# First rows and constants loaded earlier, and the modulation's columns transposed on the chip, in a hybrid RG-LRU, attention and expert layer

## What is computed

```
silu_c, silu_cc = silu(c), silu(c_ctx)
m_lat = silu_c  @ w_mod + b_mod            # 1024 x 6144
m_ctx = silu_cc @ w_mod + b_mod
sh1, sc1, g1, sh2, sc2, g2 = split(m_lat, 6)      # and sh1c, sc1c, ... of m_ctx
h_lat = normalise(x)   * (1 + sc1)  + sh1         # mean and variance over the 1024 columns
h_ctx = normalise(ctx) * (1 + sc1c) + sh1c
u, g, q, k, v = split(h @ w_in)                   # w_in: 1024 x 1792
```

## Time and profile before

| | |
|---|---|
| median of 3 runs | 2081.2 us (2080.24 to 2082.03) |
| the profiled execution | 2081.28 us |
| its span, first to last instruction | 2079.5 us |
| mean granted TensorE clock | 0.923 |
| PE busy | 1713.2 us, 82% of the span |
| DVE busy | 1464.5 us, 70% |
| ACT busy | 1066.5 us, 51% |
| DMA moved | 412.59 MB, 198 GB/s in the mean |

### The profile page before, as it was taken

The page is one execution under the profiler, slowest core; times in us unless marked ns, Lnnn a source line. Parts: engine busy times, 40 slices in busy tenths (PEclk is TensorE's granted clock), DMA queues, the critical chain, the costliest instruction groups (busy, mean ns, idle before and its releaser), DMA issues. The chain is left out here.

```text
span 2079.5 us, 76106 instructions
## 1 busy us (share of the span) xinstructions
PE 1713.2 (82%) x31174; PEld 1373.2 (66%) x31176; DVE 1464.5 (70%) x1828; ACT 1066.5 (51%) x1378; POOL 526.5 (25%) x413
## 2 busy tenths in 40 slices
PE   3488888888669997899961689986899799999947
PEld 0266666434257776455541689986899799999932
DVE  2466766388869997788878747777888636578727
ACT  2234343577558886433311535566676435456626
POOL 0000000000047777333322113231323121233213
PEclk7599999999889999899975899998999899999979
DMA  9321211367363331344326576898999748879837
GB/s 375 104 92 56 96 60 52 129 229 259 122 251 124 115 121 40 125 153 159 136 91 223 196 242 206 266 361 316 352 373 342 263 137 280 270 228 368 272 77 278
DMA packets 167293, 412.59 MB, mean 198 GB/s; under 512 B 15977, under 2 KB 24625, under 8 KB 165553
## 3 DMA queue, kind: packets, MB, share of 16 engines
q1 hardware_dynamic: 155554, 369.14, 49.4%
q0 software_dynamic: 11664, 42.47, 8.3%
HBM read 343.38 MB, written 68.19 MB: 198 GB/s over the span
## 5 line engine op out<-in xcount | busy, mean ns | idle before, releaser
L2200 PE MATMUL ps<-arena 128*128 128x64 f16 x7680 | 708.5, 195 | 53.9 <-DVE arena L2121 25.7
L2200 PEld LDWEIGHTS ps<-arena 128*128 128x128 f16 x7680 | 686.5, 99 | 62.5 <-issue 50.4
L2201 PE MATMUL ps<-arena 128*128 128x64 f16 x7680 | 708.3, 195 | 4.7 <-issue 3.9
L2202 PE MATMUL ps<-arena 128*128 128x64 f16 x7680 | 708.2, 195 | 3.9 <-issue 3.0
L2201 PEld LDWEIGHTS ps<-arena 128*128 128x128 f16 x7680 | 686.2, 99 | 6.0 <-issue 5.0
L2202 PEld LDWEIGHTS ps<-arena 128*128 128x128 f16 x7680 | 686.3, 99 | 2.8 <-issue 2.7
L2121 DVE SCALAR_TENSOR_TENSOR arena<-arena 128x2048 f16<-128x2048 f32 (+1 forms) x232 | 457.6, 2012 | 162.9 <-ACT arena L2048 95.5
L2048 ACT ACTIVATE arena<-arena 128x2048 f16<-128x2048 f32 x192 | 359.0, 1904 | 126.3 <-DMA arena<-w 80.0
L644 PE MATMUL ps<-arena 128*128 128x256 f16 (+1 forms) x1680 | 237.7, 303 | 21.1 <-DVE arena L529 21.1
L644 PEld LDWEIGHTS ps<-arena 128*128 128x128 f16 x1680 | 165.8, 100 | 87.3 <-DVE arena L529 15.2
L2015 POOL COPY ix<-gidx 128x1 int32 (+1 forms) x40 | 47.0, 1176 | 531.3 <-DVE arena L2154 531.3
(11 more groups left out here) (308 smaller groups left out, 3107.6 us busy)
## 6 DMA issues: line engine op xcount, KB each, us to landing
arena<-w SPq DMA_DIRECT2D x192, 1024.0 KB, 12.0
arena<-hT_d SPq DMA_DIRECT2D x64, 512.0 KB, 6.2
arena<-w_mod SPq DMA_DIRECT2D x16, 1536.0 KB, 8.3
h_d<-arena SPq DMA_DIRECT2D x17, 512.0 KB, 3.0
x_d<-arena SPq DMA_DIRECT2D x17, 512.0 KB, 2.6
arena<-x SPq DMA_DIRECT2D x8, 1024.0 KB, 6.2
hT_d<-arena SPq DMA_DIRECT2D x16, 512.0 KB, 3.1
arena<-x SPq DMA_DIRECT2D x16, 512.0 KB, 4.7
```

The costliest lines, as they stand in the source:

```text
L2200: pe.matmul(out, whi[lane][:, at:at + P], high, start=first, stop=False)
L2201: pe.matmul(out, whi[lane][:, at:at + P], low, start=False, stop=False)
L2202: return pe.matmul(out, wlo[lane][:, at:at + P], high, start=False, stop=last)
```

## The change

In `phase_modulation`:

- The ring's fourth slot, the raw `w_in` and the rows lie elsewhere in `arena`, so that the places of the context rows, the first x rows, the parameters and the tables are free in this phase.
- `w_in` is loaded in twelve transfers (four groups of k, of 2, 2, 3 and 1, by three ranges of columns); ScalarE starts when the groups with k = 0 to 3 have landed. The two zero transfers are issued ahead of the second round of slabs.
- The stationary side of the modulation's matmuls is padded with zeros to 32 columns, so that all 128 PSUM partitions are written, and the additions of `b_mod` run once for each half over 128 partitions, after all eight slabs. The place of the rows is zeroed first, and `b_mod` is loaded after that.
- Behind the last slab SyncE issues the context rows, the first x rows, the parameters, and the tables.
- DVE makes all eight low halves of `w_in` first, then takes the statistics of the context rows, adds `b_mod`, scales the context rows, and forms `mcol` from PSUM, where PE has put six transposes of the rows. POOL makes the first power in this phase.
- The stores to `mod_rows` are issued when the rows are done, and their landing is awaited only in the phase of the output projection.

In `phase_project` those loads, the reading back of `mod_rows`, the first norm and the small transpose are gone. A semaphore in the expert phase is replaced by one that an earlier phase used.

```diff
 def phase_modulation(nc, env):
-    a = arena_slices(arena, 0, [(f"w{j}", 2 * WIDE) for j in range(RING)] + [("rows", HALVES * NARROW), ("spare", D)])
+    ring = [arena[:, at:at + 2 * WIDE].rearrange("p (k n) -> p k n", k=2) for at in (0, 2 * WIDE, 4 * WIDE, PAR0 + 36)]
+    rows = arena[:, ROWS0:ROWS0 + HALVES * NARROW]
-    c2a = small[:, 2 * KD:4 * KD]
+    c2a = small[:, 384:384 + 32 * KD]
         def _(sp):
             sp.dma_start(c2s, g["c2"]).then_inc(c_ld, 16)
+            sp.wait_ge(rows_done, 1)
             for m in range(4):
-                sp.dma_start(rows[m], by_group[0][m]).then_inc(c_ld, 16)
+                sp.dma_start(row_of[m], by_group[0][m]).then_inc(c_ld, 16)
...
-            for dst, src in ((0, 0), (D_RNN, D), (REST, D_RNN)):
-                size = QKV if src == D else D_RNN
-                sp.dma_start(raw[:, :, dst:dst + size], w_in[:, :, src:src + size]).then_inc(win_ld, 16)
+            first = 0
+            for at, count in RAW:
+                part = arena[:, at:at + count * D_IN].rearrange("p (k n) -> p k n", k=count)
+                for dst, src in ((0, 0), (D_RNN, D), (REST, D_RNN)):
+                    size = QKV if src == D else D_RNN
+                    sp.dma_start(part[:, :, dst:dst + size], w_in[:, first:first + count, src:src + size])\
+                        .then_inc(win_ld if first < KD // 2 else win_ld2, 16)
+                first += count
+            sp.wait_ge(rows_done, 2)
+            for table in (g["h2_d"], g["x1_d"]):
+                sp.dma_start(table[SEQ:SEQ + P, :], spare).then_inc(rows_st, 16)
             for n in range(RING, RING * HALVES):
                 sp.wait_ge(mod_mm, n - RING + 1)
                 sp.dma_start(ring[n % RING], slab(n)).then_inc(wmod_ld[n % RING], 16)
-            sp.wait_ge(rows_done, 1)
-            for table in (g["h2_d"], g["x1_d"]):
-                sp.dma_start(table[SEQ:SEQ + P, :], spare).then_inc(rows_st, 16)
-            sp.wait_ge(rows_done, 1 + 4 * HALVES)
+            sp.wait_ge(later("b_pads"), START + 1)
+            sp.dma_start(first_rows(arena, 0), g["ctx_x"].rearrange("(t p) d -> p t d", p=P)).then_inc(x_ld[0], 16)
+            sp.dma_start(first_rows(arena, 1), g["x"][0:TPC * P, :].rearrange("(t p) d -> p t d", p=P)).then_inc(x_ld[1], 16)
+            sp.dma_start(arena[:, PAR0:PAR0 + C_RNN * NPAR].rearrange("p (c n) -> p c n", n=NPAR),
+                         g["rg_par"].rearrange("(c p) n -> p c n", p=P)).then_inc(tab_ld, 16)
+            for at, src in ((COS0, "cos_t"), (SIN0, "sin_t")):
+                sp.dma_start(arena[:, at:at + T_LAT * 32].rearrange("p (n d) -> p n d", d=32), g[src].rearrange("n p d -> p n d"))\
+                    .then_inc(tab_ld, 16)
+            sp.wait_ge(rows_st, 32)
+            sp.wait_ge(rows_done, 2 + HALVES)
             for m in range(4):
-                sp.dma_start(by_group[1][m], rows[m]).then_inc(rows_st, 16)
-            sp.wait_ge(rows_st, 96)
+                sp.dma_start(by_group[1][m], row_of[m]).then_inc(rows_st, 16)
...
         def _(pe):
-                            mm = pe.matmul(ps[32 * m:32 * m + 2, i, 0:NARROW], c2a[:, 2 * k:2 * k + 2],
+                            mm = pe.matmul(ps[32 * m:32 * m + 32, i, 0:NARROW], c2a[:, 32 * k:32 * k + 32],
...
+            pe.wait_ge(rows_done, 2 + HALVES)
+            for i in range(HALVES):
+                for q in range(COLS):
+                    mm = pe.transpose(ps[:, 2 + i, q * P:(q + 1) * P], rows[:, i * NARROW + q * P:i * NARROW + (q + 1) * P], g["idn"][:])
+            mm.then_inc(later("b_mcol_tr"), 1)
         def _(dve):
+            nc.vector.memset(rows, 0.0).then_inc(rows_done, 1)
+            nc.vector.memset(c2a, 0.0)
             nc.vector.memset(spare, 0.0).then_inc(rows_done, 1)
+            for k in range(KD):
+                dve.wait_ge(win_hi, 2 * k + 2)
+                for cols, (high, low) in halves:
+                    nc.vector.scalar_tensor_tensor(low[:, k, :], raw[k][:, cols], W_SCALE, high[:, k, :], ALU.mult, ALU.subtract)
+            scale = norm_rows(nc, dve, g, first_rows(arena, 0), 0, (x_ld[0], START + 16))
             dve.wait_ge(c_ld, 80)
+            dve.wait_ge(mod_mm, RING * HALVES)
             for i in range(HALVES):
-                dve.wait_ge(mod_mm, RING * (i + 1))
-                for m in range(4):
-                    nc.vector.tensor_tensor(rows[m][:, i, :], ps[32 * m:32 * m + 2, i, 0:NARROW], rows[m][:, i, :], ALU.add).then_inc(rows_done, 1)
-                for k in range(4 * i, 4 * i + 4):
-                    dve.wait_ge(win_hi, 2 * k + 2)
-                    for cols, (high, low) in halves:
-                        nc.vector.scalar_tensor_tensor(low[:, k, :], raw[:, k, cols], W_SCALE, high[:, k, :], ALU.mult, ALU.subtract)
+                part = rows[:, i * NARROW:(i + 1) * NARROW]
+                nc.vector.tensor_tensor(part, ps[:, i, 0:NARROW], part, ALU.add).then_inc(rows_done, 1)
+            scale()
+            dve.wait_ge(later("b_mcol_tr"), START + 1)
+            for s in range(2):
+                at = ps[:, 2:4, 0:NARROW].rearrange("p i (q m c) -> p c i m q", q=COLS, m=4)[:, s]
+                nc.vector.tensor_scalar(mcol[:, s, 0:12].rearrange("p (m q) -> p m q", q=COLS), at[:, 0], X_SCALE, None, ALU.mult)\
+                    .then_inc(sc_ok, 1)
+                nc.vector.tensor_scalar(mcol[:, s, 12:15], at[:, 1, 0], X_SCALE, None, ALU.mult).then_inc(sc_ok, 1)
+                nc.vector.tensor_scalar(mcol[:, s, 15:16], at[:, 1, 1, 0:1], X_SCALE, None, ALU.mult).then_inc(sc_ok, 1)
+            dve.wait_ge(sc_ok, START + 6)
+            nc.vector.tensor_scalar(mcol[:, :, KD:2 * KD], mcol[:, :, KD:2 * KD], X_SCALE, None, ALU.add).then_inc(sc_ok, 1)
```

More of the change, by code:

```diff
@@ L200, in output_weights, with first_rows, norm_columns, norm_rows @@
                                         ("wr", KD * 36), ("br", 36), ("whi", KD * D // 2), ("wlo", KD * D // 2)])
+X_FIRST = B0
+COS0 = B0 + 2 * TPC * D + 4 * (KD * CHUNK // 2) + 4 * CHUNK
+SIN0 = COS0 + T_LAT * 32
+RAW = ((15204, 2), (X_FIRST + 2 * TPC * D, 2), (SIN0 + T_LAT * 32, 3), (9216, 1))
+ROWS0 = WIN0 - 1300
+assert PAR0 >= RAW[3][0] + D_IN and RAW[0][0] + 2 * D_IN + 4 <= B0 and RAW[1][0] + 2 * D_IN + D <= COS0
+assert RAW[2][0] + 3 * D_IN <= ROWS0
+def first_rows(arena, j):
+    return arena[:, X_FIRST + j * TPC * D:X_FIRST + (j + 1) * TPC * D].rearrange("p (t d) -> p t d", t=TPC)
+def norm_columns(small):
+    return dict(mcol=small[:, 0:32].rearrange("p (s n) -> p s n", s=2),
+                st=small[:, 32:32 + 12 * TPC].rearrange("p (t a s) -> p t a s", t=TPC, a=2),
+                mv=small[:, 80:80 + 2 * TPC].rearrange("p (t s) -> p t s", t=TPC),
+                ve=small[:, 96:96 + TPC], rs=small[:, 100:100 + TPC], mh=small[:, 104:104 + TPC])
+def norm_rows(nc, dve, g, x, s, landed):
+    sem, col = g["sem"], norm_columns(g["small"])
+    stats, var_e, rstd, normed = sem("b_stats"), sem("b_var"), sem("b_rstd"), sem("b_normed")
+    st, mv, ve, rs = col["st"], col["mv"], col["ve"], col["rs"]
+    dve.wait_ge(landed[0], landed[1])
+    for t in range(TPC):
+        for a in range(2):
+            nc.vector.bn_stats(st[:, t, a, :], x[:, t, a * 512:(a + 1) * 512]).then_inc(stats, 1)
+    dve.wait_ge(stats, START + 3 * TPC * s + 2 * TPC)
+    dve.sem_inc(g["alone"], 1)
+    for t in range(TPC):
+        nc.vector.bn_aggr(mv[:, t, :], st[:, t, :, :]).then_inc(stats, 1)
+    dve.wait_ge(stats, START + 3 * TPC * s + 3 * TPC)
+    nc.vector.tensor_scalar(ve, mv[:, :, 1], EPS, None, ALU.add).then_inc(var_e, 1)
+    def scale():
+        dve.wait_ge(rstd, START + s + 1)
+        for t in range(TPC):
+            nc.vector.tensor_scalar(x[:, t, :], x[:, t, :], mv[:, t, 0:1], rs[:, t:t + 1], ALU.subtract, ALU.mult).then_inc(normed, 1)
+    return scale
 def phase_modulation(nc, env):
@@ L208, in phase_modulation @@
     HALVES = FRONT // WIDE
+    COLS = NARROW // P
     def slab(n):
@@ L214, in phase_modulation @@
     sem, arena, ps, small = g["plain_sem"], g["arena"], g["ps"], g["small"]
+    later = g["sem"]
     c_ld, silu_done = sem("a_c_ld"), sem("a_silu_done")
@@ L261, in _ @@
                 pool.sem_inc(s, START)
+            nc.gpsimd.memset(col["mh"], -0.5).then_inc(later("b_pads"), 1)
+            pool.wait_ge(later("b_pads"), START + 1)
+            pool.wait_ge(later("b_var"), START + 1)
+            nc.gpsimd.tensor_tensor(col["rs"], col["ve"], col["mh"], ALU.pow).then_inc(later("b_rstd"), 1)
         @block.scalar
@@ L489, in _ @@
         def _(pool):
-            nc.gpsimd.memset(mh, -0.5).then_inc(pads, 1)
             k_words = arena[:, KT0:V0].rearrange("p (z t) -> p z t", z=2 * NKV)
@@ L499, in _ @@
             pool.wait_ge(pads, START + 8)
-            with pool.Fori(0, LAST + 1) as s:
+            with pool.Fori(1, LAST + 1) as s:
                 pool.wait_ge(var_e, START + s + 1)
@@ L1005, in _ @@
             sp.dma_start(ow["gnc"], g["gn"]).then_inc(w_ld, 16)
```

(1 more changed line is left out.)

78 lines of the change are left out of this document (30 added, 48 removed).

## The result

In the first comparison the changed kernel took 2060.49 us (median of 5; 2054.13 to 2062.72) and the kernel before 2080.24 (median of 5; 2070.84 to 2082.03): a ratio of 0.9913, interval 0.9884 to 0.9941.

| | before, median (n) | after, median (n) | ratio | interval |
|---|---|---|---|---|
| first | 2080.24 (5) | 2060.49 (5) | 0.9913 | 0.9884 to 0.9941 |
| second | 2075.96 (29) | 2059.37 (6) | 0.9931 | 0.9915 to 0.9947 |
| third | 2068.55 (23) | 2057.06 (5) | 0.9933 | 0.9909 to 0.9957 |
| fourth | 2078.55 (15) | 2060.84 (6) | 0.9923 | 0.9906 to 0.9940 |

A forecast was written before the change was run, and what follows sets the result against it. DMA engines bound everything up to 55.3 us, then short steps follow one another. Terms from the last slab at 57.0 put the first modulated tile at 68.2 instead of 81.48, 13.3 us less: 2068.0 us, range 2064.0 to 2074.0.

The forecast's parts named there:

- the tile: Start of ScalarE's first modulated tile (L424) in the projection: 81.48 us before, forecast 68.2, 13.3 us less.
- How the numbers follow: Prediction's section on chances and range: forecast 0.79, range 2064.0 to 2074.0 us, faster by more than 4.2 us 0.95.
- Zero rows: Two 512 KB writes moved ahead of the second round of slabs: last slab +1.0 us later, bounds +0 and +1.65.
- Twelve transfers of `w_in`: Splitting the w_in load costs 0, bounds -0.5 and +2.7 us; as a rival at +2.7, 2070.7 us, chance 0.05.
- Halves: w_in conversions start near 31 us, last low half ends near 49; the second 8.10 us leave the path.
- Context rows: Loads issued directly behind the last slab: the context's 1024 KB need 2.5 us, land at 59.5 and start DVE's chain.
- the rival that loads behind the slab are served together with it: Context, x and tables hold up the last slab until 63.3: 2071.4 us, or 2074.5 if context lands last; chance 0.08.
- Additions: Adding b_mod on DVE: two of 128x384 instead of eight of 2x384, 0.58 each, 1.15 us, ending at 63.8.
- Tables: Cosine and sine loads become the wait at the first low half after L424: 2068.7 or 2072.7 us, chance 0.04.
- trail the slabs: Rival: w_in's halves still come behind the modulation slabs, returning 8.1 us: 2076 us, chance 0.01.
- The clock: PE's rise to full clock early in the projection: counted 0, with 2.9 us kept both ways.
- The slower rival: Projection stays longer at half clock: gain gone after 26.6 us more, 2086 us at 36 more; chance 0.03.

The follow-up runs named there:

- The variant: Changed kernel with the two zero-row transfers issued behind the first x rows; run three times: 13.9, 17.6 and 16.4 us less than the kernel before.
- the columns through memory: Changed kernel with loads early, but the rows stored, awaited, read back and transposed as in the kernel before: 12.3 us less than the kernel before.
- low halves early alone: Kernel before with w_in in two groups of k and all low halves ahead of the second additions: 4.3 us less than the kernel before.

## Why the prediction was wrong, and where it was right

**The step that failed** is the one from the tile to the time, under "Sum" and "How the numbers follow". The saving at the tile, 12.83 us, is within 0.5 of the 13.3 forecast. But the time was worked out as 2081.2 less that saving, as if 2081.2 held for the kernel before within the 1.8 us of the three executions that I was shown, and with nothing for what lies behind the tile ("After L424 the diff changes nothing that costs time"). Neither had a term in the range, which ended with the bounds of the front's own terms.

By the means of the first comparison the 8 us that are missing divide as follows. The kernel before took 2078.0 and not 2081.2, which is 3.2 us. The changed kernel took 2059.9, that is 18.1 less; with 12.8 at the tile, 5.3 lie behind it. The tile itself gives back 0.5. Of the 5.3 the later comparisons confirm 1.8 with an error of 0.8, whose cause is open (above); the rest is within the error of 2.6 that the difference of two means of five has here. So part of the miss is chance. The scatter is plain from the runs: the kernel before has a standard deviation of 3 to 5 us within a comparison (2062.6 to 2084.0 over all), and medians of 2068.6 to 2080.2 from chip to chip. A sign of it stood in the profile too, though only later profiles made it readable: it has the longest experts' phase of the 17. A range for a median of five should have had about 5 us more at either end, twice that error, and would have held 2060.5.

**Point by point at the front:**

- Start: b_mod issued at 1.70 (1.8 forecast), the stream 0.50 later (0.62). Right.
- Zero rows: forecast +1.0 with an upper bound of 1.65; the last slab's matmuls began at 58.17, that is 2.33 later than the start explains. The variant shows that it is the zero rows: behind x they leave the slab at 55.68. The term was 2.5 by size and rate, less 0.85 that the last slab seemed to have paid already (4.61 us behind the third against 3.76), and both parts are off. The first slabs of the round show the whole price: 46.88 is 3.17 later than 43.21 plus the start, and in the other three profiles of the change the same sum gives 2.8 to 3.1. And the 0.85 is not particular to the zero rows. In the variant, with the context rows behind it, the last slab still came 4.55 us after the third (4.37 and 4.47 in the other two profiles). With the zero rows ahead it was 3.79, 3.79, 3.96 and 4.28 in the four profiles of the change, and 4.72 with the columns through memory. What causes this lateness stays open; as a credit it was not safe.
- Twelve transfers of `w_in`: 0 forecast; the conversions of the second part begin at 39.63, 0.21 after the 39.42 of before in a stream that is 0.50 late. Right. The 2.7 us by the section "Bandwidth" of "DMA: Bandwidth & Descriptors" of the Trainium skill did not come: its rate for a transfer of 1 MB did not hold for these, one behind the other in a full queue.
- Halves: conversions at 30.32 (31 forecast) and 39.63 (40), last low half done at 49.55 (49). Right.
- Context rows: 2.54 us behind the last slab (2.5). Right, so the rival that loads behind the slab are served together with it, which put the slab at up to 63.3, fell.
- Additions 1.02 us (1.15), transposes 1.51 (1.7), columns 66.45 to 67.16, 0.71 (1.1, outside the bounds of 0.8 to 1.3): together 0.7 us cheaper, which gave back part of the zero rows' 1.3. The six small operations began 0.06 to 0.09 us apart and the last 0.18 behind the sixth, below even my lower bound. That the tile came out within 0.5 is thus in part two errors that offset each other.
- SyncE: the sine table's issue ended at 63.27, the stores at 66.01, ahead of DVE's 67.16. DVE set the end, as forecast, with a margin of 1.2 us.
- End of the phase at 67.45 (66.9), first tile at 68.65 (68.2). The recorded terms, summed from 59.5, give 66.55 for the columns' end where the text has 66.65, and 68.04 for the tile, rounded there to 68.2.
- Tables: the first low half (L599, 69.80) waited for ScalarE's tile and not for the tables, so that rival fell too; and with conversions from 30.32 and the last low half at 49.55 the halves don't trail the slabs.
- The clock: the first 72 projection matmuls took 10.32 us (10.89 before), 0.6 less, within the 2.9. Full clock was granted within the window 81 to 82, as forecast. The slower rival fell: the rest of the projection took 300.7 us against 301.2.

## What to carry to other kernels

When a stretch is bound by a full DMA queue, count every transfer that moves ahead of the awaited one with its whole size over the rate, and take nothing off for a delay whose cause is not shown. Taking work off the last engine of a phase pays only down to the next. With low halves early alone that was SyncE's wait for stores to land, 2.4 us behind DVE, and only removing the trip through memory as well set it free; with the zero rows behind x it was SyncE's issue of the stores, which took 0.6 of the 2.3 us hoped for. And a forecast of a time needs the scatter of executions as a term of its own, and one for what the change might do where it is thought to do nothing: a saving that the timeline placed to half a microsecond was forecast in a time that was 7.5 us off.

## What the runs showed of the hardware

- Which of its two levels TensorE has in the first 60 us does not follow from the program alone: 16 equal matmuls took 2.79 us in one slab and 1.50 in the next, and the same slab of the same program, the one at about 50.6 us, took 2.79 us in the changed kernel's first profile and 1.50 in its second; in the fourth all of them took 2.79. This agrees with the Trainium skill, "TensorE: Matmul & The Clock Gate", section "What's actually happening", by which the chip's look at activity runs on by itself and does not start with the kernel. In the projection full clock came 5.9 and 5.7 us after the first matmul in the two profiles of before, and 4.7, 4.2, 4.7 and 6.0 us after it in the four of after. The granted clock of a window ahead of the first record is shown as 1.00: in the kernel before the windows up to 23 us show it while the slab at 20.57 took 2.74 us, so that there the durations, not the clock column, tell the level.
- Four memsets of 128x3072 on DVE, one behind the other, took 2.62 us each and left 0.59 us of idle between them; of the three memsets of 768, 256 and 1024 columns at the start of the changed kernel the last came after 0.16 us of idle.
- The issue of 256 KB of the sine table (2048 rows of 128 bytes) took 8.26 us in the changed kernel, that of 512 KB of zero rows (128 rows of 4 KB) 0.97, both into a queue with work ahead of them. That the number of rows is the cause was not tried, and the place in the queue counts as well: with the zero rows behind x their two issues took 3.71 and 2.82 us instead of 0.97 each.
